# One-hot sums in PSUM in place of scattered expert rows, in the last layer of a two-layer diffusion backbone

## The chip, the cores and the metric

The kernel runs on 1 core of a Trainium2 chip. The metric is the device time of one execution in microseconds (us). Engines are named as in the profile: PE is TensorE (matmuls; PEld its weight loads), DVE VectorE, ACT ScalarE, POOL GpSimd, SP SyncE, which here only issues DMAs and clears semaphores.

## The reference, cut to what matters

Two layers, each an attention mixer and a mixture of experts (MoE); the output is the final RMSNorm of the latent stream. In the last layer only the 256 latent tokens go through the MoE. Each token picks 8 of 64 experts; D = 1024 and an expert's hidden width is 256.

```python
h = modulate(rms_norm(x, norm_ffn[l]), sh_f, sc_f)
x = x + g_f * moe_ffn(h, ...)
return rms_norm(x, final_norm)

# moe_ffn, for T tokens
scores = sigmoid(h @ router_w)
_, idx = top_k(scores + router_bias, 8)
gates  = s_sel / sum(s_sel) * 2.5
# for each token t and each chosen expert e:
routed[t] += gates[t, e] * ((silu(h[t] @ w_gate[e]) * (h[t] @ w_up[e])) @ w_down[e])
shared = (silu(h @ sh_gate) * (h @ sh_up)) @ sh_down
return routed + shared
```

All of it is float32. An expert's weights are 1 MB each for gate, up and down, so the 64 experts of a layer are 192 MB.

## The kernel before, in words

The kernel is a sequence of stages. A stage is one block in which each engine runs its own list of instructions in order and engines meet by semaphores; at the end of a stage (`Stage.__exit__`, L239 to L246) all engines meet, SP clears the stage's semaphores one by one (L245), and they meet again (L241).

**Routing into rounds.** `feed_forward` (L1131) is the MoE stage of both layers. Its first part computes scores, picks, gates and a plan: each expert gets a number of units of 32 rows by its rank in load, and four units make a round of 128 row slots. Layer 0 (512 tokens) has 43 rounds, layer 1 (256 tokens) has 28. Of the 28, twenty mix four tiles of 32 rows (a round begins one to three new experts, 64 in all). The shared expert is computed at the start of the stage and is added into `core.x` by `dve_shared_add` (L1290).

**A round n.** In the order of PE (L1856 to L1865): `pe_gate_up(n)` multiplies the turned rows by gate and up weights (bank n % 2); `pe_turn(n + 1, 0)` turns the first half of the next round's rows; `pe_turn_hidden(n)` turns the hidden (bank 6); `pe_turn(n + 1, 1)` the second half (the halves of x use banks 4 and 5); `pe_down(n)` computes the two halves of y (banks 2 and 3). Every fourth round `pe_info` adds a small product from which DVE computes the indices and gates of four later rounds (`dve_hot`, `dve_info`). ACT computes the silu (L1427), copies the second half of the turned x (L1407) and scales the second half of y by the gates (L1475); DVE computes the hidden (L1433), copies the first half of x (L1401) and the turned hidden (L1448) and scales the first half of y (L1468).

**Queues.** POOL fetches the rows of round n + 2 from `h_rows` in DRAM by an indirect DMA (`pool_gather`, L1330, a ring of 4 buffers `xs`), and then sends y of round n - 1 by another indirect DMA to `y_rows` in DRAM, one row for each token and pick (`pool_scatter`, L1340). SP loads the weights in order: in layer 1 a ring of 6 slots for gate and up (2 MB each, `sp_gate_up`, L1308) and of 5 for down (1 MB each, `sp_down`, L1316). A slot is loaded again when the last round that reads it has issued its product: `gu_ready` for gate and up, `down1_ready` for down. All DMAs share 16 DMA engines.

**After the rounds.** Every engine reads `longest` (`further`, L1478) and skips a fallback for experts that got more rows than planned. POOL has waited for all scatters by then. Then the stage ends. `combine` (L1869) reads the 8 rows of each of its tokens back from `y_rows` (two tiles of 4 MB), sums them on DVE and POOL, multiplies by the modulation's gate, adds to `core.x`, and normalises; `finish` (L2365) loads the final gain, multiplies and stores the output. In layer 0 the rows are read back by `combine_project`, which the change does not touch.

## Time and profile before

| | |
|---|---|
| time, three runs | 2033.0, 2040.92, 2044.33 us; median 2040.92 |
| the profiled execution | 2037.85 us, of which the span is 2036.0 |
| PE busy | 1668.2 us (82% of the span) |
| DVE, ACT, POOL busy | 582.4, 312.7, 246.8 us |
| DMA | 577.24 MB, mean 284 GB/s |
| mean granted TensorE clock | 0.92 of full speed |

Busy shares of the whole span say little here, since the stages have different limits. The changed stage is the MoE of the second layer. It starts near 1395 us; its 28 rounds run from 1445 to 1968 us and what follows them ends at 2036 us. The profile's numbers come from one execution, so a sum that is made of them is to be set against 2037.85 and not against the median.

### The profile page before, as it was taken

Reading aid. Unit: us, or ns where it says so; the run is one execution under the profiler, and the core shown is the slowest. Engines: PE = TensorE matmul, PEld = TensorE weight load, DVE = VectorE, ACT = ScalarE, POOL = GpSimd, SP = SyncE. Lnnn points to the kernel's source line nnn. Section 1 sums busy time; section 2 is a strip of 40 time slices with the busy share of each in tenths; the row PEclk is TensorE's granted clock in tenths of the full one; section 3 lists DMA queues with packets and bytes.
Section 4 is the critical chain, followed back from the end, with each engine's and each line's share of the span. In section 5 each row is a group of like instructions: output and inputs, shape, how many; then the busy total and the mean of one; then the engine's idle time right before and its main releaser. Section 6 shows DMA issues by size and latency. Waiting matters only on the chain. (4 is left out here: it accounts for less than half of the span.)

```text
span 2036.0 us, 23240 instructions
## 1 busy us (share of the span) xinstructions
PE 1668.2 (82%) x8439; PEld 761.4 (37%) x8439; DVE 582.4 (29%) x1320; ACT 312.7 (15%) x686; POOL 246.8 (12%) x229
## 2 busy tenths in 40 slices
PE   5999999989999999999992899788687767676750
PEld 2544544455434433334430344445232222222210
DVE  2122444525422222222211531753211111110105
ACT  2102333221011111111110210532010000000000
POOL 0301222100011111111110000210111100101002
PEclk7999999999999999999996899898888888887875
DMA  9414665026799999999993904004999999999934
GB/s 355 125 58 150 230 225 207 1 73 247 283 405 412 414 419 407 410 406 405 417 414 157 366 0 165 5 0 143 421 421 418 418 408 407 410 411 408 396 147 175
DMA packets 129505, 577.24 MB, mean 284 GB/s; under 512 B 19282, under 2 KB 24801, under 8 KB 78960
## 3 DMA queue, kind: packets, MB, share of 16 engines
q1 hardware_dynamic: 107248, 520.59, 64.0%
q0 software_dynamic: 21280, 52.01, 6.7%
q10 hardware_dynamic: 864, 3.15, 0.4%
q8 instruction: 69, 1.13, 0.2%
q14 instruction: 44, 0.36, 0.0%
HBM read 558.32 MB, written 41.48 MB: 295 GB/s over the span
## 5 line engine op out<-in xcount | busy, mean ns | idle before, releaser
L1419 PE MATMUL ps<-wb,pool 128*32 128x512 f32 (+2 forms) x2608 | 502.7, 619 | 71.6 <-issue 71.6
L1419 PEld LDWEIGHTS ps<-wb,pool 128*32 128x32 f32 (+2 forms) x2608 | 163.2, 127 | 367.7 <-issue 367.7
L1433 DVE TENSOR_TENSOR ffn_hid<-ffn_sg,ps 128x256 f32<-128x256 f32 x71 | 29.9, 421 | 693.7 <-ACT ffn_sg L1427 693.7
L1459 PE MATMUL ps<-pool,ffn_hidT 128*32 128x512 f32 (+2 forms) x584 | 176.2, 661 | 23.6 <-DMA hT<-in_expert_w_down_dram 12.7
L1459 PE MATMUL ps<-hT,ffn_hidT 128*32 128x512 f32 (+2 forms) x680 | 164.6, 624 | 20.2 <-DMA pool<-in_expert_w_down_dram 10.8
L2007 PE MATMUL ps<-wb,hT 128*128 128x512 f32 x320 | 141.1, 603 | 1.6 <-issue 1.6
L1427 ACT ACTIVATE ffn_sg<-ps 128x256 f32<-128x256 f32 x71 | 27.3, 384 | 586.9 <-PE ps L1419 586.9
L1459 PE MATMUL ps<-sh_wd,ffn_hidT 128*32 128x512 f32 (+2 forms) x272 | 103.9, 619 | 2.4 <-DVE ffn_hidT L1448 1.8
L1336 POOL DMA_INDIRECT pool<-h_rows,ffn_index x71 | 72.4, 1019 | 245.5 <-DVE ffn_index L1383 224.5
L1344 POOL DMA_INDIRECT y_rows<-sh_wgu,ffn_index x43 | 43.2, 1006 | 484.6 <-ACT sh_wgu L1475 470.1
L1419 PE MATMUL ps<-sh_wgu,pool 128*32 128x512 f32 (+2 forms) x256 | 78.1, 650 | 28.4 <-issue 28.4
L1393 PE MATMUL ps<-const,pool 128*128 128x128 f32 x568 | 93.0, 287 | 8.8 <-DMA pool<-h_rows,ffn_index 7.5
L1393 PEld LDWEIGHTS ps<-const,pool 128*128 128x128 f32 x568 | 76.3, 195 | 50.9 <-issue 48.7
L2007 PEld LDWEIGHTS ps<-wb,hT 128*128 128x128 f32 x320 | 61.6, 194 | 78.5 <-issue 78.5
L985 PE MATMUL ps<-wb,hT 128*128 128x512 f32 x192 | 83.4, 593 | 3.4 <-PEq L241 3.4
L1419 PE MATMUL ps<-ffn_wgu_more,pool 128*32 128x512 f32 (+1 forms) x208 | 80.0, 652 | 7.3 <-issue 7.3
L1344 POOL DMA_INDIRECT y_rows<-x_res,ffn_index x28 | 28.1, 1005 | 475.3 <-ACT x_res L1475 475.3
L948 POOL TENSOR_SCALAR attn_pn<-attn_p,attn_mx 128x256 f32<-128x256 f32 (+1 forms) x43 | 53.2, 1238 | 240.8 <-DVE attn_mx L886 239.1
L1459 PEld LDWEIGHTS ps<-pool,ffn_hidT 128*32 128x32 f32 (+2 forms) x584 | 50.9, 137 | 80.8 <-issue 80.8
L1459 PEld LDWEIGHTS ps<-hT,ffn_hidT 128*32 128x32 f32 (+2 forms) x680 | 47.4, 124 | 78.9 <-issue 78.9
L368 PE MATMUL ps<-wb,silu 128*32 128x512 f32 x384 | 54.0, 687 | 22.2 <-DMA wb<-in_ada_w_dram 18.3
L745 PE MATMUL ps<-wb,hT 128*128 128x512 f32 (+1 forms) x192 | 69.1, 521 | 1.3 <-PEq L241 1.3
(291 smaller groups left out, 1868.0 us busy)
## 6 DMA issues: line engine op xcount, KB each, us to landing
wb<-in_expert_w_gate_dram SPq DMA_DIRECT2D x108, 1024.0 KB
wb<-in_expert_w_up_dram SPq DMA_DIRECT2D x108, 1024.0 KB
pool<-in_expert_w_down_dram SPq DMA_DIRECT2D x52, 1024.0 KB
hT<-in_expert_w_down_dram SPq DMA_DIRECT2D x52, 1024.0 KB, 18.6
wb<-in_ada_w_dram SPq DMA_DIRECT2D x24, 2048.0 KB, 9.5
sh_wd<-in_expert_w_down_dram SPq DMA_DIRECT2D x24, 1024.0 KB
mix_yr<-y_rows SPq DMA_DIRECT2D x8, 2048.0 KB, 11.7
wb<-in_diff_w_in_dram SPq DMA_DIRECT2D x6, 2048.0 KB, 16.7
```

The lines of the kernel that those rows point to most:

```text
L368: mm = nc.tensor.matmul(core.ps[g:g + 32, bank, :], core.silu[:, k, :], w[:, k, :], start=k < 4, stop=k >= 4, skip_group_check=True, tile_ ...
L745: mm = nc.tensor.matmul(core.ps[:, n % 8, 0:widths[b]], lhs, rhs, start=k == 0, stop=k == KD - 1)
L948: nc.gpsimd.tensor_scalar(pn[:, n % 4, 0:nk], p[:, n % 4, 0:nk], mx[:, n % 4, 3:4], None, ALU.mult).then_inc(norm_pool, 1)
L985: mm = nc.tensor.matmul(core.ps[:, n % 6, :], core.hT[:, k, oT_at(t)], wo[:, k, :], start=k == 0, stop=k == KD - 1)
L1336: pool.indirect_dma_start(out=xs[:, s, :], out_offset=None, in_=r.h_rows, in_offset=bass.IndirectOffsetOnAxis(ap=index[:, n, 0:1], axis=0) ...
L1344: pool.indirect_dma_start(out=r.y_rows, out_offset=bass.IndirectOffsetOnAxis(ap=index[:, n, 1:2], axis=0), in_=y[:, n % 2, :], in_offset=N ...
L1393: mm = nc.tensor.transpose(core.ps[:, 4 + half, (k % 4) * P:(k % 4 + 1) * P], xs[:, s, k:D:KD], core.c("ident"))
L1419: mm = nc.tensor.matmul(core.ps[lo:lo + width, n % 2, :], xT[:, n % 2, k, lo:lo + width], w[:, k], start=k == 0, stop=k == KD - 1, skip_gr ...
L1427: nc.scalar.activation(sg[:, n % 2, :], core.ps[:, n % 2, 0:F], ACT.Silu).then_inc(silu_ready, 1)
L1433: nc.vector.tensor_tensor(hid[:, n % 2, :], sg[:, n % 2, :], core.ps[:, n % 2, F:2 * F], ALU.mult).then_inc(hid_ready, 1)
L1459: mm = nc.tensor.matmul(core.ps[lo:lo + width, 2 + half, :], hidT[:, n % 2, k, lo:lo + width], wd_at(q % DR, half, k), start=k == 0, stop= ...
L2007: mm = nc.tensor.matmul(core.ps[:, n % 6, :], core.hT[:, k, t * P:(t + 1) * P], wb[:, k, :], start=k == 0, stop=k == KD - 1)
```

## The change

It touches the second layer (`last` is true where `r.out` is given); in layer 0 all is as before but for one more wait (`sums_used`).

- y rows are no longer scattered. For each round DVE builds a one-hot matrix of slot against token (`dve_back_hot`), and PE multiplies y by it (`pe_sum`): four 128x512 matmuls that add into banks 4 to 7 over all 28 rounds. `pe_sum(n - 1)` stands behind `pe_gate_up(n)`.
- Banks 4 to 7 are thus taken. The rest shares fewer: gate/up has bank 0, both halves of y bank 1, both halves of x bank 2, the hidden and `info` bank 3. So `pe_gate_up(n)` waits for the hidden of n - 1, the second half of x for the copy of the first, the second half of y for the scaling of the first. The second turn of x now stands between the two halves of `pe_down`.
- The ring of gather buffers has 3 in place of 4; the last one holds the final gain, which SP loads behind the last weights.
- After the rounds DVE multiplies the two sums by the modulation's gate and adds them to `core.x`; the norm, the final gain and the store follow in this stage. `combine`, `finish` and `y_rows` of the layer are gone. The fallback adds its rows the same way.

```diff
+        XS = RING - 1 if last else RING
...
+        sh_bank = lambda i: 4 if i % 2 == 0 else 6 if last else 2
+        gu_bank = lambda n: 0 if last else n % 2
+        down_bank = lambda half: 1 if last else 2 + half
+        x_bank = lambda half: 2 if last else 4 + half
+        hid_bank, (info_bank, info_at) = (3, (3, F)) if last else (6, (7, 0))
...
             elif i == 1:
                 pe.wait_ge(scratch_free, 1)
+                pe.wait_ge(sums_used, 1)
...
         def pe_turn(pe, n, half):
+            if last and half == 1:
+                pe.wait_ge(xa_ready, n + 1)
+            elif n >= 1:
+                pe.wait_ge(xb_ready if last else (xa_ready, xb_ready)[half], n)
...
         def pe_gate_up(pe, n):
+            if last and n >= 1:
+                pe.wait_ge(hid_ready, n)
...
+        def pe_down(pe, n, half):
+            if half == 0:
+                for q in plan.begins(n):
+                    pe.wait_ge(d_in[q % DR], 16 * (q // DR) + 16)
+                pe.wait_ge(hidT_ready, n + 1)
+            if last and half == 1:
+                pe.wait_ge(y0_ready, n + 1)
+            elif n >= 1:
+                pe.wait_ge(y1_ready if last else (y0_ready, y1_ready)[half], n)
...
+        def dve_back_hot(dve, n):
+            if n >= 2:
+                dve.wait_ge(summed, n - 1)
+            nc.vector.tensor_scalar(back_hot[:, n % 2, :], core.c("iota")[:, 0:T], tok[:, n:n + 1], None,
+                                    ALU.is_equal).then_inc(back_ready, 1)
+
+        def pe_sum(pe, n):
+            pe.wait_ge(back_ready, n + 1)
+            pe.wait_ge(y0_ready, n + 1)
+            pe.wait_ge(y1_ready, n + 1)
+            for i in range(NT):
+                for half in range(2):
+                    mm = nc.tensor.matmul(core.ps[:, 4 + 2 * i + half, :], back_hot[:, n % 2, i * P:(i + 1) * P],
+                                          y[:, n % 2, half * 512:(half + 1) * 512], start=n == 0, stop=n == R - 1,
+                                          skip_group_check=True)
+            mm.then_inc(summed, 1)
...
+        def dve_final(dve, i):
+            rs = norm.rs
+            dve.wait_ge(norm.sq_ready, i + 1)
+            nc.vector.tensor_scalar(rs[:, 0, i:i + 1], norm.ss[:, i:i + 1], 1.0 / D, EPS, ALU.mult,
+                                    ALU.add).then_inc(norm.var_ready, 1)
+            dve.wait_ge(norm.root_ready, i + 1)
+            nc.vector.reciprocal(rs[:, 2, i:i + 1], rs[:, 1, i:i + 1]).then_inc(norm.inverse, 1)
+            dve.wait_ge(norm.inverse, i + 1)
+            nc.vector.scalar_tensor_tensor(out=core.xn[:, i, :], in0=core.x[:, tiles[i], :], scalar=rs[:, 2, i:i + 1],
+                                           in1=gain, op0=ALU.mult, op1=ALU.mult).then_inc(done, 1)
...
             @block.sync
+                if last:
+                    sp.wait_ge(xb_turned, R)
+                    sp.dma_start(gain, final_norm.rearrange("(o d) -> o d", o=1).to_broadcast([P, D])).then_inc(gain_in, 16)
                 further(sp, None, lambda b, e, n: fb_sp(sp, b, e, n))
+                if last:
+                    for i in range(NT):
+                        sp.wait_ge(done, i + 1)
+                        sp.dma_start(r.out[0, i * P:(i + 1) * P, :], core.xn[:, i, :]).then_inc(stored, 16)
+                    sp.wait_ge(stored, 16 * NT)
...
             @block.gpsimd
                     if n + 2 < R:
                         pool_gather(pool, n + 2, last_row)
-                    if n >= 1:
+                    if n >= 1 and not last:
                         pool_scatter(pool, n - 1, last_out)
...
             @block.vector
                     dve_take_hidden(dve, n)
+                    if last:
+                        dve_y(dve, n)
+                        dve_back_hot(dve, n)
...
+                if last:
+                    dve.wait_ge(summed, R)
+                    for i in range(NT):
+                        link(scaled_sum(i, y[:, i, :]))
+                        link(added(i, y[:, i, :]))
+                    dve.sem_inc(fb_free, 1)
...
             @block.tensor
                 for n in range(R):
                     pe_gate_up(pe, n)
+                    if last and n >= 1:
+                        pe_sum(pe, n - 1)
...
                     if n + 1 < R:
                         pe_turn(pe, n + 1, 0)
                     pe_turn_hidden(pe, n)
+                    if last:
+                        pe_down(pe, n, 0)
                     if n + 1 < R:
                         pe_turn(pe, n + 1, 1)
-                    pe_down(pe, n)
+                    for half in range(1 if last else 0, 2):
+                        pe_down(pe, n, half)
+                if last:
+                    pe_sum(pe, R - 1)
```

New semaphores of the stage in layer 1: `back_ready`, `summed`, `x_ready`, `gain_in`, `done`, `stored`, `sums_used`, `fb_back`, `fb_back_sum`, `fb_prod` and the five of `RowNorm`.

## Rows read from the trace of the kernel before

**Rows 1.** Busy time by stretch: us, each engine's busy us (instructions), PEclk, DMA share, GB/s.

```profile
1445.00:1968.00 523.00, 380.38 (x2505) 142.41 (x2504) 75.52 (x161) 45.66 (x83) 51.57 (x51) 0.88 0.97 397
1946.00:1950.00 4.00, 3.69 (x34) 1.47 (x27) 0.74 (x2) 0.38 (x1) 0.00 (x0) 1.00 0.44 186
1968.00:2036.00 68.00, 0.00 (x0) 0.00 (x0) 29.32 (x20) 4.15 (x8) 14.38 (x5) 0.53 0.36 148
```

**Rows 2.** Waits in the rounds: who waited for whom: us in total, times, longest.

```profile
POOL y_rows L1344 <- ACT x_res L1475: 463.5, 27, 30.9
...
PE ps L1419 <- issue: 97.0, 16, 11.1
```

**Rows 3.** Timeline of ACT: start us, us, engine, line, what [idle before <-releaser].

```profile
1452.23 0.39 ACT L1427 ACTIVATE ffn_sg<-ps 128x256 f32<-128x256 f32 x1 [11.04 <-PE ps L1419]
...
1614.99 0.39 ACT L1427 ACTIVATE ffn_sg<-ps 128x256 f32<-128x256 f32 x1 [6.36 <-PE ps L1419]
...
1627.71 0.39 ACT L1427 ACTIVATE ffn_sg<-ps 128x256 f32<-128x256 f32 x1 [6.35 <-PE ps L1419]
...
1961.67 0.38 ACT L1427 ACTIVATE ffn_sg<-ps 128x256 f32<-128x256 f32 x1 [6.32 <-PE ps L1419]
1967.48 0.69 ACT L1475 ACTIVATE x_res<-ps,ffn_gate 128x512 f32<-128x512 f32 x1 [5.43 <-PE ps L1459]
```

**Rows 4.** Timeline of all engines after the rounds.

```profile
1981.28 0.81 SPq L1886 DMA_DIRECT2D wb<-y_rows  x2
1993.80 2.29 DVE L1904 TENSOR_TENSOR wb<-wb 128x2048 f32<-128x2048 f32 x1 [27.29 <-DMA wb<-y_rows]
...
2010.50 1.06 ACT L430 ACTIVATE pool<-x_res 128x1024 f32<-128x1024 f32 x1 [42.34 <-DVE x_res L1910]
...
2013.39 0.75 DVE L446 TENSOR_SCALAR pool<-x_res,combine_rs 128x1024 f32<-128x1024 f32 x1
...
2030.09 2.36 DVE L2385 TENSOR_TENSOR pool<-pool,final_gain 128x1024 f32<-128x1024 f32 x2 [4.85 <-DMA final_gain<-in_final_norm_dram]
```

**Rows 5.** Line 1586, meeting at the block's end: engine, count, ns min/median/max, when.

```profile
L1586 DVEq DRAIN  x1: 10/10/10, 1966.7 to 1966.7; - x1
...
L1586 POOLq DRAIN  x1: 4635/4635/4635, 1972.4 to 1972.4; - x1
```

**Rows 6.** Line 245, SP clears the stage's semaphores, same columns.

```profile
L245 SPq EVENT_SEMAPHORE_RANGE_CLEAR  x69: 25/25/25, 1977.3 to 1981.0; - x69
```

**Rows 7.** Timeline of all engines at the starts of both MoE stages.

```profile
508.31 3.60 PE L1286 MATMUL ps<-sh_wd,ffn_hidT 128*128 128x512 f32 x8
...
509.52 0.22 DVE L1755 TENSOR_TENSOR ffn_hits<-ps,ffn_caps 128x64 f32<-128x64 f32 x1
...
1440.36 4.80 PE L1286 MATMUL ps<-sh_wd,ffn_hidT 128*128 128x512 f32 x8
```

**Rows 8.** Groups by line and shape, 1445 to 1968 us: count, busy us, mean ns.

```profile
L1468 DVE TENSOR_SCALAR x_res<-ps,ffn_gate 128x512 f32<-128x512 f32 x28 | 21.0, 751 | 97.4 <-PE ps L1459 97.4
...
L1401 DVE COPY pool<-ps 128x512 f32<-128x512 f32 x27 | 18.5, 686 | 0.0
...
L1448 DVE COPY ffn_hidT<-ps 128x256 f32<-128x256 f32 x28 | 11.9, 424 | 0.6 <-PE ps L1441 0.6
...
L1299 DVE TENSOR_TENSOR x_res<-ps,ffn_gate 128x1024 f32<-128x1024 f32 x1 | 1.2, 1224 | 4.8 <-PE ps L1286 4.8
```

**Rows 9.** Line 1480, the load of `longest`, same columns as rows 5.

```profile
L1480 DVEq TENSOR_LOAD <-ffn_longest x1: 319/319/319, 1965.8 to 1965.8; - x1
```

**Rows 10.** Line 241, the meeting at the end of the last stage.

```profile
L241 POOLq DRAIN  x1: 34/34/34, 2035.6 to 2035.6; - x1
```

**Rows 11.** DMA in the rounds: queue, packets, MB, engine share; issues, us to landing.

```profile
q0 software_dynamic: 7473, 15.40, 7.6%
...
pool<-h_rows,ffn_index POOLq DMA_INDIRECT x24, 10.9
```

**Rows 12.** Timeline of PE, the start of round 26.

```profile
1938.98 1.07 PE L1419 MATMUL ps<-sh_wgu,pool 128*32 128x512 f32 x2 [10.20 <-issue]
```

More of the change, by code:

```diff
@@ L1146, in feed_forward @@
     LAG = EARLY - STREAM
+    last = r.out is not None
+    XS = RING - 1 if last else RING
     with Stage(nc, f"ffn{layer}") as st:
@@ new lines, in pe_down @@
+        def pe_down(pe, n, half):
[7 more added lines that the diff above has]
+                pe.wait_ge(y1_ready if last else (y0_ready, y1_ready)[half], n)
+            for k in range(KF):
+                for q, lo, width in plan.tiles(n):
+                    mm = nc.tensor.matmul(core.ps[lo:lo + width, down_bank(half), :], hidT[:, n % 2, k, lo:lo + width],
+                                          wd_at(q % DR, half, k), start=k == 0, stop=k == KF - 1,
+                                          skip_group_check=True, tile_position=(0, lo))
+            mm.then_inc((down0_ready, down1_ready)[half], 1)
@@ L1583, in fb_pe @@
             mm.then_inc(fb_down_ready, 1)
+            if last:
+                pe.wait_ge(fb_y_ready, n + 1)
+                pe.wait_ge(fb_back, n + 1)
+                for i in range(NT):
+                    for half in range(2):
+                        mm = nc.tensor.matmul(core.ps[:, 4 + 2 * i + half, :], back_hot[:, 0, i * P:(i + 1) * P],
+                                              y[:, 0, half * 512:(half + 1) * 512], start=True, stop=True)
+                mm.then_inc(fb_back_sum, 1)
         rw_in, bias_in, wgu_in, wd_in, table_in = sw.rw_in, sw.bias_in, sw.wgu_in, sw.wd_in, sw.table_in
@@ L1640, in _ @@
                 for n in range(R):
-                    if n >= 1:
+                    if n >= 1 and not last:
                         act_y(act, n - 1)
@@ L1645, in _ @@
                         act_take_x(act, n + 1)
-                act_y(act, R - 1)
+                    if last:
+                        act_y(act, n)
+                if not last:
+                    act_y(act, R - 1)
                 further(act, None, lambda b, e, n: fb_act(act, b, e, n))
+                if last:
+                    for i in range(NT):
+                        act.wait_ge(x_ready, i + 1)
+                        norm.act_square(act, i)
+                        norm.act_root(act, i)
             @block.vector
@@ L1768, in _ @@
                     ahead = n % BATCH == 0 and b < plan.batches
-                    if n >= 1:
+                    if n >= 1 and not last:
                         dve_y(dve, n - 1)
```

198 lines of the change are left out of this document (84 added, 114 removed).

## The prediction, as it was recorded

> **What bounds the kernel now.** I read the busy time by stretch first, to see which engine is full in the stage that the change touches. From 1445 to 1968 us, the 28 rounds of the second layer, the 16 DMA engines are busy 0.97 of the time at 397 GB/s and TensorE (PE) 380 of 523 us, at a mean granted clock of 0.88; from 1968 to 2036 us PE does nothing at all and the DMA engines work a third of the time [rows 1]. So two parts with different limits stand there: rounds paced by expert weights, and a tail in which small steps follow one another. The waits of the rounds say the same: PE stands 97 us in 16 times ahead of the gate/up product with no engine to wait for (its weights have not landed), and GpSimd spends 463 us waiting to send its 27 scatters, which hurts nobody [rows 2]. In ScalarE's timeline two successive rounds that wait for no weights are 12.72 us apart, from 1614.99 to 1627.71 us [rows 3]. 28 such rounds are 356 us; those of the trace take 522 (1445.1 to 1967.4). PE thus has 5.9 us of slack a round, and whatever lengthens its round is hidden only as long as that slack lasts.
>
> **The change, tail first.** The last down product ends as ScalarE starts its half of y, at 1967.48 us [rows 3]. From there before: y, the last scatter, a read of 8 MB of rows issued at 1981.28, whose first half releases the sums at 1993.80, the final multiply from 2030.09 on and the end at 2036.0 [rows 4]. That is 68.5 us. In the 13 us ahead of the read stand a GpSimd drain of 4.6 us, from 1972.4 on [rows 5], and the clearing of the stage's 69 semaphores by SyncE (SP), from 1977.3 to 1981.0: 0.054 us each [rows 6].
> After, from the same point: ScalarE's y 0.69 and a handoff, 0.75. Then the last one-hot sum: four 128x512 f32 matmuls, each recorded as two; the shared expert's down product is four of this form and takes 3.60 us at full clock (4.80 when it begins at the lower one) [rows 7]. Then two scalings out of PSUM and two additions on VectorE (DVE), 1.23 us each as the shared expert's are, 5.0 with handoffs [rows 8]. The test of `longest` now stands on this path: DVE's load of it starts at 1965.8 and the engine reaches the block's end at 1966.7, so 0.9 [rows 5, 9]; 0.2 for the handoff. Square to reciprocal is 2.9 us (2010.50 to 2013.39, one table load in it), the norm's multiply has two tensor inputs now, so 1.2 as the final one, and the second tile follows 1.9 later (0.6 of small steps, 1.2). The store takes 3.2 from the end of the final multiply (2030.09 + 2.36) to the drain at 2035.6 [rows 4, 10]. Last, 84 semaphores (69, and 15 more by the diff) are cleared where final had 3: 4.6, and 0.3 of barriers. The sum is 24.5 us (0.75 + 3.6 + 5.0 + 0.9 + 0.2 + 2.9 + 1.2 + 1.9 + 3.2 + 4.9), against 68.5: **-44**. A second table load (1.3) or a slower PSUM read could be missing in it, and the handoffs are bare; I keep -41 to -46.
> Two things come for nothing. The gain's 0.5 MB load waits for the last turn of x, which comes ahead of the last down product, and has more than 14 us until it is used. The extra VectorE operation of the one-hot matrix (128x256 f32) is bounded by the 0.42 us of a PSUM copy of that size from above and zero from below [rows 8] and stands behind y, while PE runs its second down half and the next gate/up; if this cover failed it would be 0.4 x 28 = 12 us.
>
> **The rounds: the DMA side.** The GpSimd queue takes 7.6% of 16 engines over 523 us, 39.7 us, for 24 gathers and 27 scatters of the same rows; the scatters' part is 27/51, **21 us**; by bytes, 15.4 MB x 27/51 at 397 to 420 GB/s, 20 [rows 11]. If the weights alone set the pace this is the gain: -20. It is the ceiling, unless small writes also slow reads beyond their share; nothing here shows that.
> Gathers: with 3 buffers instead of 4 and no scatter ahead of it in GpSimd's queue, a gather goes out when its buffer has been turned, three rounds ahead of its use; its landing takes 10.9 us in the trace [rows 11], under one round. Nothing. If that cover went, PE would wait the difference in each round.
>
> **The rounds: the PE side.** Each round gains one one-hot sum. Back to back its eight records cost 3.43 of the 3.60 us (the last one's tail overlaps); from below it is 3.1, as it fills the 0.3 us in which PE waits for `hid`; from above 4.8, the row at the lower clock [rows 7]. I take 3.1, since the sum stands behind a gate/up that has warmed the clock. The single banks add two waits. The turned hidden is copied by DVE behind its copy of x: 0.69 + 0.42 and handoffs after the first turn, of which the hidden's turn covers 0.45, leaving 0.8 where the second turn of x stood before. And the second down half waits until DVE has taken the first: 0.75 + 0.15, of which the second turn of x, moved there, covers 0.6, leaving 0.3 [rows 8]. Queued behind these waits is all of PE; for them wait, in turn, the releases of down slots, hence SP, hence the DMA. Together 4.2 us a round, 16.9 in place of 12.7, or 473 us in 28. Bounds are 3.1 (both waits hidden) and 7.5 (4.8 and nothing covered).
> 473 is less than 522 - 20 = 502, so weights stay the pace on the mean, but 5.9 us of slack become 1.0. What does not average out: the last two rounds. Round 26 starts its gate/up at 1938.98 after a wait of 10.20 us and round 27 follows it without one, up to 1967.4 [rows 3, 12]. Their lengthening is exposed in full: 4.2 + 3.8 = +8. And slots are released later in each round, while rounds need one to three new experts, 3 to 9 MB, 8 to 23 us of supply, against an even 16.9 of work; a round that needs one expert now overruns its supply by 9 us instead of 5. The six gate/up and five down slots hold 17 MB, 41 us of supply, so most of it is caught, not all. Ends for this: 0, and +38 (of the 27 spacings between the 28 silus, 1452.23 to 1961.67, 11 are under 14.6 us [rows 3]; 4.2 exposed in each, less the 8 already counted). I take +5, close to the low end, because the DMA share stays at 0.97 over the stage [rows 1]. Stage: -20 + 8 + 5 = **-7**.
>
> The clock: in the stretch from 1946 to 1950 the granted clock is 1.00 (2.4 GHz), while round 26's first records, after the idle 10.20 us, are 1.07 us long, where eight at the full clock fill 3.60 [rows 1, 7, 12]. The change shortens such idle stretches, so part of the +8 can come back; I count nothing. The Trainium skill (TensorE: Matmul & The Clock Gate, "HAM oscillation — how this bites in real kernels") says that a loop whose DMA waits exceed a limit restarts at the half clock on each pass; the trace agrees, with the 1.07 us. By it round 26 without its wait would get back at most half of the 7 us between 1938.98 and 1946, some 3 us, and the sum would be 1984.
>
> The first layer: `sums_used` comes at 509.74, at the end of the subtraction at L1755, while the first shared down product (508.31 + 3.60) still runs [rows 7]. The new wait is met before PE reaches it: 0.
>
> **The sum.** From the profiled execution: 2037.85 (span 2036.0 and 1.85 around it) - 44 - 7 = **1987 us**. That execution is 3 us under the median of the three runs shown, 2040.92; the range covers the difference.
>
> **Rivals.** (a) *PE becomes the pace.* If the waits on single banks are covered by nothing (0.9 + 0.9 + 0.9 instead of 1.1), a round is 18.5 us and 28 are 518; with the waits for weights that the uneven rounds still cause (some 17 us) the stage is 13 longer: 2037.85 - 44 + 13 = 2007. For it: only 1.0 us of slack is left. Against: the diff puts the turns of x and of the hidden into these gaps. The Trainium skill (Perfetto Trace Analysis, "Matmuls") says that independent groups should rotate through different PSUM banks so that one's evacuation overlaps the next one's matmuls; that speaks against this change, and no row of before shows the rotation missing. (b) *Supply alone counts*: slots catch all, and the last rounds' lengthening is paid by shorter waits: -20, so 1974. For it: DMA share 0.97; against: rounds 26 and 27 run back to back. (c) *Slower: the added matmuls run at 1.2 GHz.* Place: PE in the rounds. The price is the 14.5 us of a round's matmul work doubled for the share of time at the low clock. Before, the mean clock of 0.88 is a share of 0.24 [rows 1]; if it stayed, rounds would be 16.9 + 3.5 = 20.4 us, stage 571, +49: 2043. It decides from 20.2 us a round on, where stage and tail cancel ((522 + 44)/28). Against it: the low clock follows the long waits, and these go.
>
> **Numbers.** Forecast 1987 with 0.56 (own range 1978 to 1998), (a) 0.21, (b) 0.19, (c) 0.04. The range 1974 to 2008 leaves out (c), the far side of (a) and what lies below (b), under 0.2. A change of 0.5% is what a measurement of this kernel can tell; faster than 2030.7 us is all but (c) and a hair of (a): 0.95, within 0.5% 0.02, slower 0.03.
>
> **What would show it.** Tail right: no DMA of y rows, last down product to end about 25 us, 4.6 of them clearing semaphores after the store has landed. Rounds right: spacing of silus that wait for nothing 16.9 us, PE clock above 0.95, GpSimd queue under 4%, last down product at 1960 (b: 1947; a: 1980). (c) would show 592 ns records turned to 1062 ns in the sums. I am wrong if the stage moves by more than 20 us either way, or if the silu spacing exceeds 18 us.

## The result, and the profile after

The changed kernel takes 1973.14 us (median; 1969.06 to 1975.59), beside 2041.66 for the kernel before in the same session (2033.0 to 2044.33): the ratio is 0.9675, interval 0.9652 to 0.9698. The profiled execution took 1975.1 us with a span of 1973.3; before it was 2037.85 and 2036.0. Of the 62.7 us between the spans, 44.0 are the tail and 24.9 the rounds; they add to 68.9, and 6.2 go the other way, because the rounds began later in this execution: the first silu of the stage is at 1458.42 against 1452.23 [rows 3]. Next to nothing changed ahead of it (one wait in the first layer, the banks of the shared expert), and in the executions profiled for this study it lies anywhere between 1443.95 and 1460.79. So stages are compared below by their own lengths, from the first silu to the start of ScalarE's last half of y. One of the six executions of the kernel with split sums (below) took 2697.96 us at a granted clock of 0.63, and its median here is that of the five others, 1969.05 (with it 1970.69, from which a later expectation starts).

First, busy time by stretch of the kernel after: us, each engine's busy us (instructions), PEclk, DMA share, GB/s.

```profile
1450.00:1949.00 499.00, 444.22 (x2724) 171.12 (x2722) 83.23 (x195) 45.31 (x83) 26.81 (x24) 0.98 0.97 400
1930.00:1935.00 5.00, 4.78 (x32) 1.48 (x32) 0.54 (x2) 1.27 (x2) 0.00 (x0) 1.00 0.62 236
1935.00:1940.00 5.00, 5.00 (x22) 1.64 (x19) 0.26 (x1) 0.38 (x1) 0.00 (x0) 1.00 0.01 3
1949.00:1973.00 24.00, 3.67 (x8) 1.44 (x8) 8.02 (x10) 4.35 (x8) 0.00 (x0) 0.69 0.11 44
```

Against [rows 1] the DMA engines are as full as they were (0.97), and TensorE (PE) is now nearly full as well, 444 of 499 us, at a granted clock of 0.98. The last weights land by 1935; what follows is PE's own.

PE's waits in 1445 to 1950 us: who waited for whom, us in total, times, longest.

```profile
PE ps L1492 <- DVE ffn_hidT L1477: 21.4, 20, 1.1
PE ps L1448 <- issue: 16.3, 5, 6.1
PE ps L1492 <- DVE x_res L1529: 7.5, 27, 0.8
```

The 97 us in 16 waits for weights [rows 2] are 16.3 us in 5. In their place stand the two waits that the single banks make: for VectorE's (DVE's) copy of the turned hidden (L1477), and for DVE to take the first half of the down product (L1529).

ScalarE's timeline, start us, us, engine, line, what [idle before <-releaser], the rows that answer to [rows 3]:

```profile
1458.42 0.38 ACT L1456 ACTIVATE ffn_sg<-ps 128x256 f32<-128x256 f32 x1 [11.73 <-PE ps L1448]
...
1494.33 0.38 ACT L1456 ACTIVATE ffn_sg<-ps 128x256 f32<-128x256 f32 x1 [6.35 <-PE ps L1448]
...
1511.18 0.38 ACT L1456 ACTIVATE ffn_sg<-ps 128x256 f32<-128x256 f32 x1 [6.34 <-PE ps L1448]
...
1922.22 0.38 ACT L1456 ACTIVATE ffn_sg<-ps 128x256 f32<-128x256 f32 x1 [6.31 <-PE ps L1448]
...
1939.32 0.38 ACT L1456 ACTIVATE ffn_sg<-ps 128x256 f32<-128x256 f32 x1 [6.31 <-PE ps L1448]
...
1948.79 0.69 ACT L1538 ACTIVATE x_res<-ps,ffn_gate 128x512 f32<-128x512 f32 x1 [9.08 <-PE ps L1492]
```

1494.33 to 1511.18 is 16.85 us, a round that waits for nothing (12.72 before). From 1458.42 to 1948.79 the rounds take 490.37 us; before, 1452.23 to 1967.48, 515.25. That is -24.9.

PE's timeline in one free round shows what the 4.1 us more are:

```profile
1904.99 3.70 PE L1510 MATMUL ps<-x_res,rw 128*128 128x512 f32 x8
1908.53 0.60 PE L1418 MATMUL ps<-const,pool 128*128 128x128 f32 x4
1908.97 0.40 PE L1470 MATMUL ps<-const,ffn_hid 128*128 128x128 f32 x2
1910.45 0.62 PE L1492 MATMUL ps<-pool,ffn_hidT 128*32 128x512 f32 x2 [1.08 <-DVE ffn_hidT L1477]
...
1913.24 0.62 PE L1492 MATMUL ps<-pool,ffn_hidT 128*32 128x512 f32 x2 [0.22 <-DVE x_res L1529]
```

The one-hot sum occupies PE from 1904.99 to 1908.53; then 1.08 us of waiting for the hidden's copy (forecast 0.8) and 0.22 between the halves (0.3). Those are 4.8 us; what the round has less is mainly PE's wait for the hidden, 0.5 us in the round from 1614.99 to 1627.71 before, which the sum now fills.

The DMA queue of GpSimd in 1450 to 1950 us (packets, MB, share of 16 engines), which was at 7.6% [rows 11]:

```profile
q0 software_dynamic: 3603, 7.17, 3.8%
```

And the tail, all engines, from the sum behind the last y on; under it, in a fence of their own, the meeting at the block's end and SP's clears (count, ns min/median/max, when):

```profile
1949.62 3.67 PE L1510 MATMUL ps<-x_res,rw 128*128 128x512 f32 x8 [0.88 <-ACT x_res L1538]
...
1953.33 1.22 DVE L1517 TENSOR_TENSOR x_res<-ps,ffn_gate 128x1024 f32<-128x1024 f32 x1 [6.32 <-PE ps L1510]
...
1957.11 1.23 DVE L1521 TENSOR_TENSOR x_res<-x_res 128x1024 f32<-128x1024 f32 x1
1959.40 1.06 ACT L430 ACTIVATE pool<-x_res 128x1024 f32<-128x1024 f32 x1 [9.93 <-DVEq L1907]
...
1960.57 1.28 ACT L435 ACT_TABLE_LOAD   x1
...
1962.30 1.29 DVE L1550 SCALAR_TENSOR_TENSOR pool<-x_res,ffn_rs,pool 128x1024 f32<-128x1024 f32 x1
...
1964.12 1.28 DVE L1550 SCALAR_TENSOR_TENSOR pool<-x_res,ffn_rs,pool 128x1024 f32<-128x1024 f32 x1
```

```profile
L241 POOLq DRAIN  x1: 41/41/41, 1968.4 to 1968.4; - x1
...
L245 SPq EVENT_SEMAPHORE_RANGE_CLEAR  x84: 25/25/25, 1968.5 to 1973.0; - x84
```

From 1948.79 to the end at 1973.3 is 24.5 us against 68.5 [rows 3, 4]. Each small step has nothing beside it, and the 84 clears are the longest single one.

### The profile page after: what moved, and what is told of

It is laid out like the page before. It is cut to its first block and busy times, and to the rows that moved or that the text cites. A ratio compares the mean times of both kernels' runs of the same rounds, so it can differ in the third digit from the quotient of the medians.

```text
span 1973.3 us, 23640 instructions
## 1 busy us (share of the span) xinstructions
PE 1739.5 (88%) x8663; PEld 793.9 (40%) x8663; DVE 568.7 (29%) x1345; ACT 312.3 (16%) x686; POOL 207.1 (10%) x197
## 3 DMA queue, kind: packets, MB, share of 16 engines
HBM read 549.94 MB, written 26.80 MB: 292 GB/s over the span
## 5 line engine op out<-in xcount | busy, mean ns | idle before, releaser
L1448 PE MATMUL ps<-wb,pool 128*32 128x512 f32 (+2 forms) x2608 | 486.7, 600 | 19.3 <-issue 19.3
L1492 PE MATMUL ps<-pool,ffn_hidT 128*32 128x512 f32 (+2 forms) x584 | 165.9, 604 | 23.9 <-DVE ffn_hidT L1477 10.8
L1492 PE MATMUL ps<-hT,ffn_hidT 128*32 128x512 f32 (+2 forms) x680 | 157.7, 599 | 19.7 <-DVE ffn_hidT L1477 14.8
L1510 PE MATMUL ps<-x_res,rw 128*128 128x512 f32 x224 | 103.1, 603 | 0.9 <-ACT x_res L1538 0.9
L1433 ACT COPY pool<-ps 128x512 f32<-128x512 f32 x71 | 41.6, 585 | 296.5 <-PE ps L1418 296.5
L1448 PE MATMUL ps<-ffn_wgu_more,pool 128*32 128x512 f32 (+1 forms) x208 | 73.9, 622 | 5.7 <-issue 5.7
L1426 DVE COPY pool<-ps 128x512 f32<-128x512 f32 x71 | 48.8, 688 | 90.3 <-PE ps L1418 89.9
L1448 PE MATMUL ps<-sh_wgu,pool 128*32 128x512 f32 (+2 forms) x256 | 72.7, 602 | 1.6 <-issue 1.6
L1492 PEld LDWEIGHTS ps<-pool,ffn_hidT 128*32 128x32 f32 (+2 forms) x584 | 45.3, 127 | 69.4 <-issue 62.6
```

Source lines behind the costliest of these rows:

```text
L1426: nc.vector.tensor_copy(xT[:, n % 2, 0:4, :].rearrange("p k c -> p (k c)"), core.ps[:, x_bank(0), :]).then_inc(xa_ready, 1)
L1433: nc.scalar.copy(xT[:, n % 2, 4:8, :].rearrange("p k c -> p (k c)"), core.ps[:, x_bank(1), :]).then_inc(xb_ready, 1)
L1448: mm = nc.tensor.matmul(core.ps[lo:lo + width, gu_bank(n), :], xT[:, n % 2, k, lo:lo + width], w[:, k], start=k == 0, stop=k == KD - 1, sk ...
L1492: mm = nc.tensor.matmul(core.ps[lo:lo + width, down_bank(half), :], hidT[:, n % 2, k, lo:lo + width], wd_at(q % DR, half, k), start=k == 0 ...
L1510: mm = nc.tensor.matmul(core.ps[:, 4 + 2 * i + half, :], back_hot[:, n % 2, i * P:(i + 1) * P], y[:, n % 2, half * 512:(half + 1) * 512], ...
```

## The experiments

The stretch is from the first silu to the start of the last y of the profiled execution; "free" is the distance of silus that wait for no weights; "weights" is PE's time of waiting for gate/up weights in the rounds. The stretch repeats closely where the rounds are the same: 490.37 (after), 489.99 (after again) and 490.17 (with other clears), 487.9 and 488.1 for the pair with split sums. The ratios are to the kernel before in the same session, whose own median lay between 2037.99 and 2042.24 us from session to session.

| kernel | median us | ratio (interval) | stretch | free | weights |
|---|---|---|---|---|---|
| before | 2041.66 | 1 | 515.3 | 12.7 | 97.0 |
| after | 1973.14 | 0.9675 (0.9652 to 0.9698) | 490.4 | 16.9 | 16.3 |
| before, no scatters | 2005.0 | 0.9817 (0.9801 to 0.9834) | 486.2 | 12.7 | 89.0 |
| after, with scatters | 2000.23 | 0.9807 (0.9786 to 0.9828) | 517.5 | 16.9 | 34.9 |
| after, no sums | 1970.66 | 0.965 (0.9634 to 0.9666) | 484.6 | 13.7 | 72.5 |
| after, double sums | 2053.6 | 1.0052 (1.0034 to 1.007) | 565.1 | 20.3 | 2.7 |
| before, plain writes, 8.4 MB | 2022.68 | 0.9929 (0.991 to 0.9947) | 503.7 | 12.7 | 98.4 |
| before, plain writes, 14.7 MB | 2033.22 | 0.9975 (0.9959 to 0.9991) | 515.2 | 12.7 | 105.4 |
| before, empty scatters | 2012.03 | 0.9876 (0.9853 to 0.9898) | 487.5 | 12.7 | 88.2 |
| before, full scatters | 2042.84 | 1.0002 (0.9984 to 1.002) | 515.7 | 12.7 | 100.2 |
| after, split sums | 1969.05 | 0.9678 (0.966 to 0.9696) | 487.9 | 15.8 | 34.4 |
| after, split sums and clears | 1960.34 | 0.9625 (0.9603 to 0.9647) | 488.1 | 15.8 | 34.9 |
| after, clears alone | 1966.46 | 0.9643 (0.9616 to 0.9669) | 490.2 | 16.9 | 16.3 |
| after again | 1972.85 | 0.9684 (0.9663 to 0.9705) | 490.0 | 16.9 | 15.9 |

**The parts of the change, one at a time.** The tail had come out as forecast and the rounds not: -24.9 for -7. My theory after the result was that either the scatters had cost more than their share of the DMA engines, or the lengthening of PE's rounds was hidden better than I had said. Four kernels tell these apart. The first is the kernel before without its scatters (the read-back then takes other data, so that the tail keeps its form):

```
-                    if n >= 1:
+                    if n >= 1 and layer == 0:
                         pool_scatter(pool, n - 1, last_out)
 ...
-        y_view = r.y_rows.rearrange("(t p k) d -> t p k d", p=P, k=TOP_K)
+        y_view = a["expert_w_down"][1][0:8].rearrange("e f d -> (e f) d").rearrange(...)
```

> The kernel before, with the 28 scatters of the second layer left out; the read-back after the rounds takes 8 MB of other data, so the output is wrong and the tail keeps its form. Theory A (scatters cost the weights their share of the DMA engines and nothing more, 21 us by the queue's 7.6%): the stretch from the first gate/up to the last down product goes from 522 to 502 us, total -20 to -24 (the drain of the GpSimd queue may also shrink). Theory B (scatters hold the weights up beyond their share): the stretch falls by 28 us or more. Theory C (engine work counts, not the DMA): less than 10 us.

The second is the changed kernel with the scatters back, beside the sums (`if n >= 1 and not last` becomes `if n >= 1`, with the wait for `scattered` in `dve_y` and `act_y`, and a wait for the last scatter ahead of the tail):

> The changed kernel, which also scatters y to DRAM in each round as the kernel before did (nothing reads it). The stretch from the first gate/up to the last down product took 497 us in the changed kernel's profile. Theory A (DMA supply paces, scatters cost their share): 518, total +21 us and some 3 for the last scatter's landing. Theory B: 525 or more. Theory C (after the change TensorE is the pace, 28 rounds of 16.9 us are 474 of the 497): a part of the scatters' traffic hides, +5 to +14 us.

The third leaves the sums of rounds 1 to 26 out, the fourth does each twice:

```
+            if 0 < n < R - 1:
+                pe.sem_inc(summed, 1)
+                return
```

```
-            for i in range(NT):
-                for half in range(2):
-                    mm = nc.tensor.matmul(core.ps[:, 4 + 2 * i + half, :], ...
+            for twice in range(2):
+                for i in range(NT):
+                    for half in range(2):
+                        mm = nc.tensor.matmul(core.ps[:, 4 + 2 * i + half, :], ...
```

> The changed kernel with the one-hot sums of rounds 1 to 26 left out (only the first and the last are computed, so the output is wrong). Waits that the single banks add are kept. Free rounds are 13.5 us apart (16.9 less 3.4), which against 12.7 before is the price of the single banks alone: 0.8. Theory A (supply paces): the stretch stays within 5 us of 497. Theory C (TensorE paces): it falls by 10 to 20 us, down to what the weights allow.

> The changed kernel with each one-hot sum computed twice (the routed part is doubled, so the output is wrong). A free round is 16.9 + 3.4 = 20.3 us and 28 of them are 568, more than any supply, so both theories A and C expect the stretch at 568 to 575 us and +72 to +80 in total. If the records of the sums grew longer than 0.6 us (lower clock) it would be more; if TensorE had hidden slack within a round, less than +60.

Measured: taking the scatters from before gives -29.0 us in the rounds (515.3 to 486.2), giving them back to after +27.1 (490.4 to 517.5). Both ways they are dearer than the 20 to 21 us that the queue's share had. The sums cost 5.8 us (484.6 to 490.4), and the single banks nothing that can be told from zero: their free round is 1.0 longer than before's (13.7 to 12.7), and the stretch is 1.6 shorter. At 20.3 us a round PE is the pace and every microsecond counts: +74.7 for 27 rounds of 3.4 to 3.5 us more, 2.8 each after what slack was left. So the price of PE's round is a curve: 484.6 us at 13.7, 487.9 at 15.8, 490.4 at 16.9, 565.1 at 20.3. It should bend near the 17.3 us (484.6 / 28) that the weights need on the mean; that is an estimate, since no run lies between 16.9 and 20.3.

Most of the rest of the -37 us of the first kernel's median is in its tail, 62.7 us in place of 68.5: no last scatter has to land.

Stretches of three of the four, in the same columns as above (before without scatters; after without sums; after with double sums; the last two for 1500 to 1600 us):

```profile
1470.00:1930.00 460.00, 344.34 (x2342) 131.67 (x2342) 67.22 (x144) 42.86 (x78) 21.73 (x22) 0.90 1.01 415
```

```profile
1500.00:1600.00 100.00, 76.17 (x556) 26.00 (x558) 16.53 (x37) 9.56 (x17) 7.17 (x6) 0.90 1.01 420
```

```profile
1500.00:1600.00 100.00, 93.54 (x554) 36.55 (x554) 14.38 (x34) 8.06 (x15) 5.58 (x5) 1.00 0.85 341
```

With double sums the DMA share falls to 0.85: the weights now wait for slots. In the two others it is full. The granted clock is 1.00 where PE idles least (busy 93.5 of 100 us), though it does most work there: the fear behind rival (c), sums at 1.2 GHz, has the sign of the coupling wrong.

**What in the scatters costs 29 us.** Three kernels take the scatters' place, and in a fourth every row is stored. The first writes from ScalarE's queue, in each round, 585 columns of all 128 rows, as many bytes as the scatters store:

```
+        def act_write(act, n):
+            act.wait_ge(y0_ready, n + 1)
+            act.wait_ge(y1_ready, n + 1)
+            dst = r.y_rows.rearrange("(b p) d -> b p d", p=P)[n % 16][:, 0:WRITE]
+            act.dma_start(dst, y[:, n % 2, 0:WRITE]).then_inc(written[n % 2], 16)
```

> The kernel before without the layer-1 scatters, and with its read-back taken from rows of another tensor, as in the run that measured 2005.0 us, but ScalarE's queue writes in each round 585 columns of the 128 rows of y straight into y_rows: 28 x 128 x 585 x 4 bytes = 8.4 MB, as many bytes as the scatters store (the sums are left out of y_rows, so the output differs). It asks what of the 28 to 29 us that the scatters cost is the traffic and what is their being row by row through GpSimd's queue. Theory A (the traffic takes its share of the 16 DMA engines, whatever queue it is in): 8.4 MB at the 397 to 412 GB/s of the rounds are 20 to 21 us, so the rounds stretch by about 20 us against the run without scatters (486.2 -> 506) and the median is 2025. Theory B (any stores cost their share and some 8 us more, because loads and stores mixed run slower): 486.2 -> 514, median 2033. Theory C (what is dear is the indirect form, with its short packets; straight rows are cheaper than their bytes): rounds stretch by under 15 us, median under 2020. q of ScalarE shows the packets in their length.

503.7 us, 17.4 more than without, and the median 2022.68: A, a little under its figure. Plain writes cost slightly less than their bytes; they are not what makes a scatter dear. Of the next two kernels the first keeps the scatters but lets them store nothing (its edit follows), and the second writes all 1024 columns plainly:

```
-                last_row, last_out = pool.to_reg(T - 1), pool.to_reg(T * TOP_K - 1)
+                last_row, last_out = pool.to_reg(T - 1), pool.to_reg(T * TOP_K - 1 if layer == 0 else 0)
```

> The kernel before with its 28 layer-1 scatters issued as they are, but with the bound of their indices lowered to row 0, so that no row of them (at most one) is stored, and the read-back taken from rows of another tensor as in the run without scatters (2005.0 us; its rounds took 486.2 us against 515.3 with scatters and 503.7 with plain writes of the same 8.4 MB). The sums' source is gone, so the output differs. It asks where the 11.6 us are that scatters cost beyond plain writes of as many bytes. Theory A (the indirect form itself: descriptors of 128 rows a round, the skipped ones as short packets too, each scatter some 0.4 us of the weights' time): rounds 486.2 -> about 498, median about 2017. Theory B (what is dear is storing single rows at scattered places, a scatter that stores nothing is free): rounds within 3 us of 486.2, median 2005 to 2008. Theory C (the skipped rows move their 4 KB too, as the counter of written HBM bytes has it, 14.7 MB and not 8.4): about 515, median 2034.

> As the run with plain writes of 585 columns, but with all 1024: 14.7 MB, the bytes that the counter of written HBM bytes shows for the scatters (the output differs in the same way). Theory A (a plain write costs its bytes at the rate of the rounds: 17.4 us for 8.4 MB): 486.2 + 30.5 = 517 us for the rounds, median about 2036. Theory B (a 4 KB row per packet is as dear as a 2.3 KB one, the price is by the packet): rounds about 504, median about 2023.

Empty scatters add 1.3 us to the rounds (B): neither GpSimd's work nor the packets of 4 bytes are the price. Their median is 7 us above that of the kernel without scatters, measured in another session; 4.8 of it are a longer tail (67.5 us against 62.7): GpSimd's drain at the block's end takes 4.6 us again, where it took 2.3 without scatters. And 14.7 MB of plain writes cost 29.0 us (A: forecast 30.5), as much as scatters of 8.4 MB. The counter of written HBM bytes, on which theory C had leaned, shows 41.48 MB with real, empty and full scatters alike, against 26.80 without: it counts what was asked for.

What is left is where the stored rows go, or which engine carries them. A scatter that stores all of its 128 rows, at rows in order:

```
+            else:
+                nc.vector.tensor_scalar(index[:, lo:hi, 1], core.c("iota")[:, 0:P * m:P], row_of[:, 0:1], None,
+                                        ALU.add).then_inc(index_ready, 1)
```

> The kernel before with its 28 layer-1 scatters, but every one stores all its 128 rows (the indices are 512 rows in order, again and again), 3584 rows and 14.7 MB in place of the 2048 rows and 8.4 MB of the routed tokens (the other 1536 rows of a round are padding and go out as packets of 4 bytes); read-back of another tensor, so the output differs. Rounds without scatters 486.2 us, with 28 empty scatters 487.5, with the real ones 515.3, with plain writes of the same 8.4 MB 503.7 and of 14.7 MB 515.2. Theory A (a scatter's rows go to the 16 DMA engines by their place among the 128, and the padding stands at fixed places, the end of each expert's rows, so that some engines store 28 x 8 rows as they would in the full case and the weights wait for them: the load is uneven): filling the padding adds nothing to the fullest engine, rounds 515 to 518 us. Theory B (a row stored by a scatter costs 27.7 us / 2048 rows = 13.5 ns, whatever its place): 487.5 + 3584 x 13.5 ns = 536 us. Theory C (what is dear is the random target row; rows in order cost as plain writes do, evenly spread): also 515 to 518, so this run tells B from the two others, not A from C.

515.7 us: 1536 more rows a stage, 6.3 MB, for 0.4 us. B (536) is out. Between A and C two rows decide, each for 1470 to 1930 us. First the DMA share and GB/s (last columns) before, with full scatters, and with plain writes of 14.7 MB:

```profile
1470.00:1930.00 460.00, 333.83 (x2190) 126.59 (x2182) 65.04 (x140) 41.44 (x75) 47.55 (x47) 0.88 1.00 412
```

```profile
1470.00:1930.00 460.00, 336.06 (x2199) 127.95 (x2192) 63.98 (x138) 40.16 (x73) 48.76 (x49) 0.88 1.01 419
```

```profile
1470.00:1930.00 460.00, 329.41 (x2168) 124.71 (x2166) 64.99 (x140) 41.06 (x74) 21.81 (x22) 0.87 1.01 419
```

The real scatters move 412 GB/s where the same queue moves 419 with all rows stored: 1.7% of 515 us, 8.6 us in which bytes could have moved and did not. Then GpSimd's queue: before, without scatters, and with full ones.

```profile
q0 software_dynamic: 7047, 14.73, 8.3%
```

```profile
q0 software_dynamic: 3292, 6.47, 3.7%
```

```profile
q0 software_dynamic: 7056, 19.98, 10.9%
```

The scatters' 8.26 MB took 4.6% of the engines, 0.56% per MB; the full ones' 13.51 MB 7.2%, 0.53% per MB. Rows at random places are at most a few per cent slower (C gives 1 us of the 8). What is left is A: some engines carry more of the stored rows than the others, and a weight transfer, spread over all 16, lands when its slowest share does.

How uneven can be worked out from the routing, by a count and not by a run. The reference's inputs give the 64 experts of this layer 111 down to 4 tokens, and each sits in its own places, 32 to a unit, filled from the unit's start. Over the 28 rounds the first eight places of the 128 are stored 208 of 224 times, the last eight never. The Trainium skill (DMA: Bandwidth & Descriptors, "The descriptor swizzle") says that a transfer of 128 partitions goes to the engines by partition, four rows and the four that stand 32 further on to one engine. By that rule the fullest engine stores 202 of the stage's rows, the emptiest 16, and an even split were 128; from the plain writes' 29.0 us for 224 rows an engine, 202 rows are 26.2 us, and with the 1.3 of the empty scatters 27.5, where an even split would give 16.6 + 1.3 = 17.9. The runs (27.1 and 29.0) stand with the first. That a row goes to its engine by its place is nothing that a row of the trace shows, since its packets carry no engine; the page states it for rows written into SBUF, and here they are read from it.

Counts of the packets and landings that the traces hold bear A out, though. Each scatter raises its semaphore by 16, and the last of these steps comes 1.33 us after the first before (median of the 28 scatters), 0.68 us with full scatters and 0.58 with empty ones. By the count above the fullest engine of a round stores eight rows more than the emptiest in the median round, and eight packets of 160 ns are 1.28 us. From 1470 to 1915 us fewer than 16 packets are in flight for 28.9 us before, and for 8.6 and 9.1 with full scatters and with 14.7 MB of plain writes. And the 4 KB packets of GpSimd's queue, gathers and scatters, take 160.4 ns on the mean before and 160.2 with the rows in order, so that a random target row costs nothing that can be told; C is out. How many of the 27 to 29 us the unevenness makes is still the estimate's figure: no run spreads the same rows evenly.

**What is still to be had.** The changed kernel's PE waits 1.08 us a round for the hidden's copy, and its tail spends 4.6 us on clears. Half of the sums moved into that wait:

```
                     pe_gate_up(pe, n)
                     if last and n >= 1:
-                        pe_sum(pe, n - 1)
+                        pe_sum(pe, n - 1, (0,))
 ...
                     pe_turn_hidden(pe, n)
+                    if last and n >= 1:
+                        pe_sum(pe, n - 1, (1,))
```

> The changed kernel with the eight sum matmuls of a round in two halves: tile 0 behind gate_up(n), tile 1 behind turn_hidden(n), where TensorE waits 1.1 us for VectorE's copy of the hidden. Theory A (TensorE's round is what is left of the change's cost): free rounds go from 16.9 to about 15.9 us, and the stretch from first silu to last y gets shorter by 1 to 4 us (the run without the sums bounds it at 5.8). Theory B (the weights' landing sets the stretch, TensorE's round only the catching up behind its gaps): free rounds 15.9 us, the stretch within 1 us, the median within 1.5 us of the changed kernel's.

PE's waits in its rounds:

```profile
PE ps L1448 <- issue: 34.4, 7, 6.8
PE ps L1492 <- DVE x_res L1530: 8.0, 28, 0.9
```

The wait for the hidden is gone and free rounds are 15.8 us; of the 27 x 1.05 = 28 us so won, 18 turn into waits for weights (16.3 to 34.4), the granted clock goes from 0.98 to 0.96, which is 2% of PE's 444 busy us, and the stretch gets 2.5 shorter. That is A's range. In time the two kernels are not told apart: the ratios are 0.9678 and 0.9675.

Then the clears as well, dealt out to four engines at each stage's end:

```
-                @block.sync
-                def _(sp):
-                    for s in self.sems:
-                        sp.sem_clear(s)
+                def clearing(i):
+                    def _(eng):
+                        for s in self.sems[i::4]:
+                            eng.sem_clear(s)
+                    return _
+                block.sync(clearing(0))
+                block.vector(clearing(1))
+                block.scalar(clearing(2))
+                block.tensor(clearing(3))
```

> The same, and the clearing of a stage's semaphores at its end is dealt out to SP, VectorE, ScalarE and TensorE instead of SP alone. The last stage's clears took SP 4.6 us behind the last output's landing, with nothing beside them. Theory A (each clear costs 0.054 us of its engine and four engines do them side by side): the tail from last y to the end goes from 24.5 to about 21 us, and each earlier stage's end is shorter by up to 3 us where the clears are on the path: 1960 to 1968 in all. Theory B (the clears share one path, or are hidden in all stages but the last): tail 24.5 us, or 21 and nothing elsewhere: 1968 to 1973.

The tail gave only 1.6 us of the forecast 3.5 (22.9), and yet the median fell by 8.7 (1969.05 to 1960.34). So the clears were run by themselves, beside the changed kernel once more:

> The changed kernel with the stage-end clears of semaphores dealt out to four engines and nothing else. With the split sums this ran at 1960.3 us against 1970.7 without, though its profile showed only 1.6 us at the tail. Theory A (the clears are on the path at every stage's end: 1.6 us at the last, 1 to 2 at layer 0's 80-odd, under 1 at the others, 4 to 6 in all): median 1967 to 1969.5. Theory B (the split sums and the clears together give what neither gives alone, or the 10 us were chance of the executions): within 2 us of the changed kernel in this call. Theory C (ten us are the clears' own, by the start of every stage's DMAs): 1962 to 1965.

> The changed kernel itself on the chip of this call, as the measure of what a median moves from call to call: 1970 to 1976 us, and silu of round 0 anywhere from 1446 to 1461 us.

The clears of the first layer's end and of the last stage, changed kernel:

```profile
L245 SPq EVENT_SEMAPHORE_RANGE_CLEAR  x73: 25/25/49, 1099.4 to 1103.8; - x73
```

```profile
L245 SPq EVENT_SEMAPHORE_RANGE_CLEAR  x84: 25/25/25, 1965.6 to 1970.1; - x84
```

and dealt out, last stage:

```profile
L245 SPq EVENT_SEMAPHORE_RANGE_CLEAR  x21: 25/25/35, 1958.6 to 1959.8; - x21
L245 ACTq EVENT_SEMAPHORE_RANGE_CLEAR  x21: 41/41/41, 1958.6 to 1960.2; - x21
L245 DVEq EVENT_SEMAPHORE_RANGE_CLEAR  x21: 54/54/56, 1958.6 to 1960.3; - x21
L245 PEldq EVENT_SEMAPHORE_RANGE_CLEAR  x21: 56/56/56, 1958.7 to 1961.1; - x21
```

21 clears take SP 1.2 us, ScalarE 1.6, DVE 1.7 and PE 2.4, 0.06 to 0.12 us each: PE is the dear one, and the last step is 2.4 instead of 4.6 us. In the medians the clears alone give 6.4 us (1972.85 to 1966.46), with the split sums 8.7; the first is a rough figure, since the intervals of its two ratios (0.9616 to 0.9669, 0.9663 to 0.9705) still touch. The stage ends agree with a gain on the way: in the two profiles the last clears of the early stages lie 1.0 us apart at 53 us, 3.2 at 379.5, 5.9 at 1103.8 (1097.9 with four engines) and 7.6 at 1396. But the start of the rounds moves by more than that between executions, so the split of the gain over the stages rests on one profile each and stays open. Of the expectations the one for 4 to 6 us (A, 1967 at the lowest) is nearest for the clears alone, missed by half a us; for both together the 1960 of A came true with a smaller tail than it had. The version with both is the fastest of the study: 0.9625 (0.9603 to 0.9647), by the ratios 10 us below the changed kernel.

## Why the prediction was right, and where it was not

**The tail, -44: right**, 68.5 to 24.5, and right in its terms: y and handoff 0.83 (0.75), sum 3.7 (3.6), DVE's four operations 5.0, to the square 1.06 (1.1), square to multiply 2.90 (2.9), clears 4.6. No cover failed: the gain's load was issued at 1930 and awaited by nobody.

**The scatters, -20: mis-sized; -29.0 by the kernel before, +27.1 by the one after.** The step said that the queue's share was the ceiling "unless small writes also slow reads beyond their share; nothing here shows that". The writes do not make the reads' packets longer (the weights' 8 KB packets take 316.1 ns on the mean before, 315.2 without scatters); they lie unevenly on the engines, as far as the runs show, and the share, a mean over 16, cannot show it. Plain writes of the same bytes cost 17.4.

**The last two rounds, +8: 6.2 of them came**, and 2.1 went back. Two kernels with the same start show it: before without scatters begins at 1458.40, after at 1458.42. PE's timeline of the former, round 26:

```profile
1914.85 1.07 PE L1419 MATMUL ps<-sh_wgu,pool 128*32 128x512 f32 x2 [9.04 <-issue]
```

and ScalarE's:

```profile
1924.28 0.38 ACT L1427 ACTIVATE ffn_sg<-ps 128x256 f32<-128x256 f32 x1 [17.73 <-PE ps L1419]
...
1944.61 0.69 ACT L1475 ACTIVATE x_res<-ps,ffn_gate 128x512 f32<-128x512 f32 x1 [7.12 <-PE ps L1459]
```

It waits 9.0 us for round 26's weights, until 1914.85. The changed kernel comes to that round without a wait, its rounds being longer, and its silu is at 1922.22, 2.1 us earlier. The granted clock says why: the kernel that had idled runs at 0.77 in 1915 to 1925, the other at 1.00.

```profile
1915.00:1925.00 10.00, 9.87 (x68) 2.94 (x63) 0.30 (x1) 0.38 (x1) 0.00 (x0) 0.77 0.96 399
```

```profile
1915.00:1925.00 10.00, 10.00 (x75) 3.82 (x72) 0.42 (x1) 1.07 (x2) 0.00 (x0) 1.00 0.94 378
```

From that silu to the last y it is 26.6 us against 20.3, the 6.2. The prediction had named this gain and counted nothing for it; the 3 us of its sentence on the Trainium skill (TensorE: Matmul & The Clock Gate, "HAM oscillation — how this bites in real kernels") was nearer.

**Late release of slots, +5: wrong, 0.** The last weights that round 26 needs land at 1914.5 us in the one kernel and at 1914.9 in the other. With 16.9 us of work against 17.3 of supply the rings of weights catch what a round is late. Without the sums PE's waits for weights are, from 1461 to 1946 us,

```profile
PE ps L1448 <- issue: 72.5, 12, 8.9
```

and with them 16.3 in 5. So 56 us of the sums are paid out of waits; PE's busy time rises only from 370.9 to 436.2 us, at a granted clock of 0.98 in place of 0.92, where 26 sums of 3.5 us are 91; and 5.8 us lengthen the stretch. The sum of the rounds is then -29.0 + 6.2 - 2.1 = -24.9, as measured, and it meets rival (b) of 1974 by luck: (b) had -20 and no lengthening, the runs -29 and +4.2.

**Free round 16.9: right** (16.85), and in its parts: the single banks alone make it 1.0 us longer (12.7 to 13.7, forecast 1.1), the sum another 3.1 (3.1). So was the clock above 0.95 (0.98) and GpSimd's queue under 4% (3.8%). The one-hot matrix on DVE is 0.34 us and hidden, as said.

**Rivals.** (a), PE as the pace: not at 16.9 us, but with the double sums, at 20.3 us, it is, and the clock then is 1.00. (c) is refuted by that same run: nearly the time it had named (2053.6; it had 2043 at 20.4 us), by longer rounds and not by a slower clock. The Trainium skill's advice to rotate PSUM banks (Perfetto Trace Analysis, "Matmuls") agrees with the 1.0 us a round that the single banks took from PE, and there they were hidden: it speaks of the engine, not of the bound.

1987 was forecast, and the profiled execution came at 1975.1, the median at 1973.14. From 1987 to 1975.1 it is -9 for the scatters, -5 for the slots and -4 for the last rounds, and +6 for an execution that began its rounds later. The forecast's own range, 1978 to 1998, did not hold it, and the whole range ends at 1974, between the two figures. The prediction had also said that it was wrong if the stage moved by more than 20 us: it moved by 24.9. So its account of the tail and of the free round is right, and its account of the stage is not: two of the three terms, the scatters and the slots, failed, both to the same side.

## What to carry to other kernels

Where transfers set the pace, price a transfer by its fullest DMA engine and not by its share: an indirect one whose valid rows stand at fixed places loads the engines unevenly, and here 8.4 MB were as dear as 14.7. Work added to an engine with slack costs little until its round meets the supply's (16.9 against 17.3 us: +5.8; 20.3: +80), and filling its idle time gives some of it back through the clock. And a chain at the end of a program is worth reading step by step: it could be summed to 0.1 us from rows of other stages, and its bookkeeping (84 clears, 4.6 us) is a step like any other.

## What the runs showed of the hardware

- A scatter whose indices are out of bounds still sends packets, of 4 bytes and some 9 ns: GpSimd's queue sent 7199 packets with 6.89 MB from 1470 to 1930 us, and 3292 with 6.47 MB without scatters. 28 such scatters of 128 rows cost 1.3 us of the weights' time. The HBM counter of written bytes has them at full size (14.7 MB more, with 8.4, 0 or 14.7 MB stored).
- Padding rows came free: 2048 or 3584 rows stored, 515.3 and 515.7 us. The other way round, spreading the valid rows evenly over the 128 places would by the count above have been worth some 9 us in the kernel before (27.5 less 17.9, an estimate). The first layer still gathers and scatters padded rounds. It wasn't tried.
- A semaphore's clear costs 0.055 us on SP alone (84 in 4.6 us); with four engines at it side by side, 0.06 on SP and up to 0.12 on PE.
- A scatter in the last round, even one that stores nothing, lengthens the tail by 4.8 us (67.5 against 62.7).
